# The MLP's last product as rows of tokens, and the context's values inside the mixer's first units

## The reference, cut to what matters

```python
# end of the first block; x is the sum after its mixer
h2 = rms_norm(x, norm_mlp_pre)
u = relu(h2 @ w_mlp_in)                                  # 1024 -> 4096
x = x + rms_norm((u * u) @ w_mlp_out, norm_mlp_post)     # 4096 -> 1024
# second block
mod, mod_k = silu(c) @ mod_w + mod_b, silu(c_ctx) @ mod_w + mod_b   # shift, scale, gate
hk = rms_norm_2(ctx, norm_g) * (1 + scale_k) + shift_k   # 256 context tokens
h = rms_norm_2(x, norm_g) * (1 + scale) + shift          # 1024 tokens
vk = hk @ w_in[:, :512]                                  # the context's values
_, state_k = rglru(vk, lp, 0)                            # gives only a start state
y, _ = mix(h, lp, state_k, pool_grid)                    # four branches, then w_out
x = x + gate * y
return rms_norm_2(x, final_g)
```

## Time and profile before

| what | us |
|---|---|
| median of 3 runs | 3014.23 |
| the profiled execution, its own time | 3017.82 |
| its span | 3016.0 |
| TensorE busy | 2786.5 (92%) |
| VectorE busy | 1413.4 (47%) |
| ScalarE busy | 954.2 (32%) |
| mean granted TensorE clock | 0.967 |

### The profile page before, as it was taken

The page is one execution under the profiler, slowest core; times in us unless marked ns, Lnnn a source line. Parts: engine busy times, 40 slices in busy tenths (PEclk is TensorE's granted clock), DMA queues, the critical chain, the costliest instruction groups (busy, mean ns, idle before and its releaser), DMA issues. The chain is left out here.

```text
span 3016.0 us, 35043 instructions
## 1 busy us (share of the span) xinstructions
PE 2786.5 (92%) x14772; PEld 2166.3 (72%) x14772; DVE 1413.4 (47%) x1638; ACT 954.2 (32%) x1324; POOL 121.4 (4%) x185
## 2 busy tenths in 40 slices
PE   6999998999989899999999999998499989998987
PEld 5867776666756676678888888886377778867776
DVE  2165443344142235944434343234647678842943
ACT  4142112243122445533324232121445622223022
POOL 0001110000000200100111100000000000000000
PEclk9989999999999999999999999998699999999999
DMA  2121101111111103642333322112221121113231
GB/s 102 42 73 40 33 30 47 62 40 31 47 48 60 50 27 98 206 159 70 98 95 93 112 85 86 47 49 84 87 67 49 36 70 56 49 42 123 77 123 65
DMA packets 67399, 215.68 MB, mean 72 GB/s; under 512 B 7752, under 2 KB 12648, under 8 KB 66736
## 3 DMA queue, kind: packets, MB, share of 16 engines
q1 hardware_dynamic: 52848, 159.76, 16.4%
q0 software_dynamic: 14400, 53.75, 5.2%
HBM read 177.83 MB, written 35.65 MB: 71 GB/s over the span
## 5 line engine op out<-in xcount | busy, mean ns | idle before, releaser
L281 PE MATMUL psum<-mixer_in,weights_parts 128*128 128x512 f32 x2112 | 504.2, 399 | 19.3 <-PEq L184 16.3
L281 PEld LDWEIGHTS psum<-mixer_in,weights_parts 128*128 128x128 f32 x2112 | 398.1, 189 | 118.7 <-issue 17.8
L439 PE MATMUL psum<-hidden,weights_parts 128*128 128x512 f32 x1536 | 436.4, 426 | 32.3 <-ACT early_gate L463 14.6
L439 PEld LDWEIGHTS psum<-hidden,weights_parts 128*128 128x128 f32 x1536 | 288.1, 196 | 116.3 <-issue 32.3
L248 DVE TENSOR_TENSOR weights_parts<-weights_raw,weights_parts 128x1024 fp32r<-128x1024 f32 (+2 forms) x186 | 200.4, 1077 | 355.9 <-ACT weights_parts L232 355.9
L281 PE MATMUL psum<-mlp_hidden,weights_parts 128*128 128x512 f32 x1536 | 352.2, 391 | 0.0
L281 PEld LDWEIGHTS psum<-mlp_hidden,weights_parts 128*128 128x128 f32 x1536 | 288.5, 188 | 63.1
L281 PE MATMUL psum<-mlp_in,weights_parts 128*128 128x512 f32 x1440 | 330.4, 391 | 0.5 <-DVE weights_parts L248 0.5
L281 PEld LDWEIGHTS psum<-mlp_in,weights_parts 128*128 128x128 f32 x1440 | 270.4, 188 | 60.0 <-DVE weights_parts L248 0.9
L281 PE MATMUL psum<-hidden,weights_parts 128*128 128x512 f32 x1200 | 277.5, 393 | 8.8 <-PEq L633 3.4
L232 ACT CAST weights_parts<-weights_raw 128x1024 fp32r<-128x1024 f32 (+2 forms) x186 | 172.9, 930 | 324.5 <-PE psum L281 244.9
(11 more groups left out here) (464 smaller groups left out, 3192.1 us busy)
## 6 DMA issues: line engine op xcount, KB each, us to landing
weights_raw<-in_w_in SPq DMA_DIRECT2D x73, 512.0 KB, 3.6
weights_raw<-in_w_mlp SPq DMA_DIRECT2D x64, 512.0 KB, 3.6
mod_weights<-in_mod_w POOLq DMA_DIRECT2D x80, 256.0 KB, 3.7
weights_raw<-in_w_gate SPq DMA_DIRECT2D x32, 512.0 KB, 3.7
gate_scratch<-early_gate SPq DMA_DIRECT2D x64, 256.0 KB, 2.0
gate<-gate_scratch POOLq DMA_DIRECT2D x32, 512.0 KB, 3.9
weights_raw<-in_w_out SPq DMA_DIRECT2D x20, 512.0 KB, 3.7
x_tokens<-in_x SPq DMA_DIRECT2D x4, 1024.0 KB, 8.1
```

The source lines that it names most:

```text
L281: mm = nc.tensor.matmul(c.psum[:, bank + h, 0:cols], c.parts[:, s, wp, at], moving(k, xp, h), start=(n < halves), stop=(n >= halves * (3 * ...
L439: mm = nc.tensor.matmul(c.psum[:, bank, :], c.parts[:, s, wp, at], self.hidden[:, k, xp, h * HALF:(h + 1) * HALF], start=(k == 0 and n == ...
```

## The change

The MLP's `gemm` ends after 56 units, with the hidden channels of the fourth chunk, which now lie in `mixer_in`. The last eight units become `mlp_rows`, a block in the form of `merged_rows`: the product in rows of tokens, and beside it the sum with `y` (turned back by TensorE, "own", copied by ScalarE, and added by VectorE), the post norm, the residual, the store, the pre norm, the turn to channels ("turn"), the modulation ("moved", eight operations of 128x128 in PSUM) and the two parts of the mixer's input. The rows overwrite the columns of `mixer_in` that they came from. The first token half of the mixer's units 0 and 1 is multiplied at the end of the block. `context_values` and `add_residual` go. The context is normed at the head of `project_and_recur`, turned between the second halves of units 0 and 1, and its product is made behind each of the units 0 to 3. The recurrence's gate weights are loaded in two halves. `mixer_out` only adds and gates; the final residual is added in rows in `final_norm`, where the squares are summed too.

In `gemm`, for units 0 and 1 that were begun in the block before:

```diff
+def second_halves():
+    last = [second_half(0)]
+    if between:
+        between(pe)
+    last.append(second_half(1))
+    for u in range(2):
+        mm = beside(pe, u) if beside else last[u]
+        mm.then_inc(c.unit_done, 1)
```

In `mlp_rows` the weights' splitting, the loads (the residual's rows go through three slots) and `mean_square` (square with a running sum, then root) are as in `merged_rows`. `inverse` waits for the root and takes the reciprocal; `normed` is a ScalarE copy scaled by it. Where the turns stand in TensorE's program, SP's loop, ScalarE's and VectorE's programs, and TensorE's waits:

```diff
+at = {(2, 3): [("turn", 0)], (2, 6): [("own", 2)], (2, 7): [("turn", 1)]}
+for b in range(3, BLK):
+    at[b, 6], at[b, 7] = [("own", b)], [("turn", b - 1)]
...
+for b in blocks:
+    if b == BLK - 1:
+        sp.wait_ge(vecs.sem, vecs.value(f"sum{b}"))
+        sp.dma_start(y[:, 4:6, :], t["ctx"].rearrange("(b p) d -> p b d", p=P)).then_inc(
+            c.ctx_loaded, 16)
+    sp.wait_ge(vecs.sem, vecs.value(f"added{b}"))
+    store(c, sp, t["x_second"][:, b, :], rows(b))
+    if b + 3 < BLK:
+        sp.wait_ge(c.scratch_stored, c.stored)
+        sp.wait_ge(act.sem, act.value(f"normed{b}"))
+        load(b + 3)
+sp.wait_ge(c.scratch_stored, c.stored)
...
+def turned_high(b):
+    a.wait_ge(vecs.sem, vecs.value(f"moved{b}"))
+    nc.scalar.copy(hidden[:, :, 0, columns(b)], turned(b)).then_inc(
+        act.step(f"high{b}"), 1)
...
+def own_rows(b):
+    a.wait_ge(pes.sem, pes.value(f"own{b}"))
+    nc.scalar.copy(y[:, :, columns(b)], turned(b)).then_inc(
+        act.step(f"own{b}"), 1)
+def norm_first(b):
+    a.wait_ge(vecs.sem, vecs.value(f"sum{b}"))
+    mean_square(1, b, result(b), w[:, 0, 0, :])
+def norm_second(b):
+    a.wait_ge(vecs.sem, vecs.value(f"added{b}"))
+    mean_square(2, b, rows(b), w[:, 0, 0, :])
...
+for b in blocks:
+    if b > 1:
+        own_rows(b)
+    norm_first(b)
+    if b > 1:
+        turned_high(b - 1)
+    if b == BLK - 2:
+        a.wait_ge(pes.sem, pes.value("parts_free"))
+        next_high(0)
+    norm_second(b)
+    if b == 1:
+        turned_high(0)
+    a.wait_ge(vecs.sem, vecs.value(f"inverse2_{b}"))
+    nc.scalar.activation(normed, rows(b), ACT.Copy,
+                         scale=rstd[:, 1, b:b + 1]).then_inc(
+                             act.step(f"normed{b}"), 1)
+    if b == BLK - 2:
+        next_high(1)
+turned_high(BLK - 1)
```

```diff
+def whole(b):
+    v.wait_ge(c.unit_done, u0 + b + 1)
+    v.wait_ge(act.sem, act.value(f"own{b}"))
+    tt(result(b).rearrange("p (k n) -> p k n", k=KT),
+       result(b).rearrange("p (k n) -> p k n", k=KT), y[:, :, columns(b)],
+       ALU.add).then_inc(vecs.step(f"sum{b}"), 1)
+def residual(b):
+    inverse(1, b)
+    stt(result(b), result(b), rstd[:, 0, b:b + 1], gain[:],
+        ALU.mult, ALU.mult).then_inc(vecs.step(f"scaled{b}"), 1)
+    v.wait_ge(x_loaded[b % 3], 16 * (b // 3 + 1))
+    v.wait_ge(vecs.sem, vecs.value(f"scaled{b}"))
+    tt(rows(b), rows(b), result(b), ALU.add).then_inc(vecs.step(f"added{b}"), 1)
+def moved(b):
+    v.wait_ge(pes.sem, pes.value(f"turn{b}"))
+    for k in range(KT):
+        nc.vector.tensor_scalar(turned(b)[:, k, :], turned(b)[:, k, :],
+                                times[:, k, 0:1], plus[:, k, 0:1], ALU.mult,
+                                ALU.add).then_inc(vecs.step(f"moved{b}"), 1)
+def turned_low(b):
+    v.wait_ge(act.sem, act.value(f"high{b}"))
+    tt(hidden[:, :, 1, columns(b)], turned(b),
+       hidden[:, :, 0, columns(b)].bitcast(F32),
+       ALU.subtract).then_inc(vecs.step(f"low{b}"), 1)
...
+v.wait_ge(gain_loaded, 16)
+for b in blocks:
+    whole(b)
+    if b > 1:
+        moved(b - 1)
+    residual(b)
+    if b == 1:
+        moved(0)
+    elif b:
+        turned_low(b - 1)
+    inverse(2, b)
+    if b == 1:
+        turned_low(0)
+    if b == BLK - 2:
+        for s in range(2):
+            low(KT + s, c.parts[:, s, 1, 0:D], c.raw[:, s, 0:D],
+                c.parts[:, s, 0, 0:D])
+moved(BLK - 1)
+turned_low(BLK - 1)
```

```diff
+def own(b):
+    if b >= 2:
+        p.wait_ge(vecs.sem, vecs.value(f"low{b - 2}"))
+    for k in range(KT):
+        last = nc.tensor.transpose(turned(b)[:, k, :], y[:, k, columns(b)],
+                                   c.ident[:])
+    last.then_inc(pes.step(f"own{b}"), 1)
...
+def turn(b):
+    p.wait_ge(act.sem, act.value(f"normed{b}"))
+    for k in range(KT):
+        last = nc.tensor.transpose(turned(b)[:, k, :], normed[:, columns(k)],
+                                   c.ident[:])
+    last.then_inc(pes.step(f"turn{b}"), 1)
...
+own(0)
+own(1)
...
+for b in range(2, BLK):
+    p.wait_ge(vecs.sem, vecs.value(f"added{b - 2}"))
+    for k in range(KT):
+        for kind, n in at.get((b, k), []):
+            do[kind](n)
+        last = product(b, k)
+        if (b, k) == (BLK - 1, 1):
+            last.then_inc(pes.step("parts_free"), 1)
+    last.then_inc(c.unit_done, 1)
...
+for u in range(2):
+    p.wait_ge(c.low_ready, u0 + KT + u + 1)
+    p.wait_ge(vecs.sem, vecs.value(f"added{BLK - 2 + u}"))
+    p.wait_ge(vecs.sem, vecs.value("low3"))
+    for k in range(KT):
+        if u and k == 5:
+            turn(BLK - 1)
+        for n, (wp, xp) in enumerate(((0, 0), (0, 1), (1, 0))):
+            mm(ps[:, 2 * u, :], c.parts[:, u, wp, columns(k)],
+               hidden[:, k, xp, 0:HALF], start=(k == 0 and n == 0),
+               stop=(k == KT - 1 and n == 2))
```

In `project_and_recur` ScalarE and VectorE first do for the context what lines 2916 to 2945 did, with the rows in `y`, and go on with the rate operations. TensorE:

```diff
+def ctx_turn(pe):
+    pe.wait_ge(vecs.sem, vecs.value("ctx_scaled1"))
+    for k in range(KT):
+        for b in range(2):
+            mm = nc.tensor.transpose(ctx_turned(k)[:, b * P:(b + 1) * P],
+                                     ctx_rows[:, b, k * P:(k + 1) * P], c.ident[:])
+    mm.then_inc(pes.step("ctx_turned"), 1)
+def ctx_product(pe, u):
+    if u >= MIX:
+        return None
+    if u >= 2:
+        pe.wait_ge(ctx_kept, u)
+    for k in range(KT):
+        if u == 0:
+            pe.wait_ge(vecs.sem, vecs.value(f"ctx_low{max(k, 1)}"))
+        for n, (wp, xp) in enumerate(((0, 0), (0, 1), (1, 0))):
+            mm = nc.tensor.matmul(c.psum[:, ctx_banks[u], 0:CTX],
+                                  c.parts[:, u % 2, wp, k * P:(k + 1) * P],
+                                  ctx_parts[:, k, xp, :], start=(k == 0 and n == 0),
+                                  stop=(k == KT - 1 and n == 2))
+    return mm
```

```diff
+def scale(act, u, s, result, act_count, dve_count, q, j):
+    act.wait_ge(c.dve_done, dve_count(u))
     nc.scalar.activation(one(final, u), one(y, u), ACT.Copy,
-                         scale=c.vectors[:, bass.ds(u + g0, 1)]).then_inc(c.act_done, 1)
-def add_all(dve, u, s, result, act_count, dve_count, q, j):
+                         scale=gate[:, bass.ds(u, 1)]).then_inc(c.act_done, 1)
+def add(dve, u, s, result, act_count, dve_count, q, j):
     nc.vector.tensor_tensor(one(y, u), one(y, u), result, ALU.add).then_inc(c.dve_done, 1)
```

In `final_norm` TensorE turns blocks 0 to 7 into four pairs of banks, ScalarE takes square and root of each added row; VectorE and SP:

```diff
+v.wait_ge(gain_loaded, 16)
+for b in range(BLK + 1):
+    if b < BLK:
+        v.wait_ge(pes.sem, pes.value("turned", b))
+        v.wait_ge(rows_loaded[b], 16)
+        nc.vector.tensor_tensor(rows[:, b, :], rows[:, b, :],
+                                c.banks(2 * (b % 4)), ALU.add).then_inc(
+                                    vecs.step(f"added{b}"), 1)
+    if b:
+        n = b - 1
+        v.wait_ge(act.sem, act.value("root", n))
+        nc.vector.reciprocal(rstd[:, n:b], ss[:, n:b]).then_inc(
+            vecs.step(f"inverse{n}"), 1)
+        v.wait_ge(vecs.sem, vecs.value(f"inverse{n}"))
+        nc.vector.scalar_tensor_tensor(
+            y[:, n, :], rows[:, n, :], rstd[:, n:b], gain[:], ALU.mult,
+            ALU.mult).then_inc(vecs.step(f"out{n}"), 1)
...
-for b in range(BLK):
-    sp.wait_ge((vecs if b % 2 else act).sem, rows_done(b))
+sp.dma_start(gain[:], t["gain_rows"][3].partition_broadcast(P)).then_inc(
+    gain_loaded, 16)
+for b in blocks:
+    sp.wait_ge(vecs.sem, vecs.value(f"out{b}"))
     store(c, sp, t["out"][b * P:(b + 1) * P, :], y[:, b, :])
```

625 lines of the change are left out of this document (261 added, 364 removed).

## The result

The changed kernel takes 2975.39 us (median of four, 2972.37 to 2978.36) against 3015.07 us before (median of four, 3012.39 to 3017.64): 39.7 us less, ratio 0.9871 with a 95% interval of 0.9859 to 0.9883. The forecast was 2968 with a range of 2955 to 2987 and a chance of 0.93 for faster: time and sign are inside, the middle was 7 us too low. The two profiled executions differ by more than the medians, 3016.0 - 2970.5 = 45.5 us of span: the one of before (3017.82) lay above its median, the one of after (2972.37) was the fastest of its four.

The account below looks back on a forecast made before the run. TensorE mostly waits in the serial chain `add_residual` and `context_values`. Up to unit 2, 165.3 against 212.6 us (-47.3), end +1.5, total -45.8: 2972 for the profiled execution, less 3.6 to the median, 2968; range 2955 to 2987.

Parts of the forecast that it names:

- Blocks 0 and 1: Row stage's first two blocks: 27.8 us, bounds 24 and 33; block 2 starts at 30.8, after block 0's norm chain.
- Block 2: Irregular row block: 12.8 + 0.9 for two turns + 3.0 waiting at "own" for block 0's low part = 16.7 us.
- Period: Row blocks 3 to 7: 12.8 us each, 10.98 for the product plus sixteen transposes, if two waits are met.
- Rival B: Row blocks: per-block chain longer than the block's product, 1 to 3 us per block for six blocks, 2974 to 2986; chance 0.20.
- Rival F: Mixer's head: context's part stays exposed; 2.4 in the sum, wholly exposed 8 more, 2976; chance 0.04.
- Stage: Whole row stage to the next block's start: product ends at 111.7, then 15.5 for the end, 127.2 us.
- Head: Mixer's start up to unit 2: 23.2 us, including a new 4.6 wait for the weights' split behind the rate operations.
- Clock: Slow clock after four stops (block 2's start, its "own", the barrier, unit 2): 4 us together, between 0 and 7.
- Rival C: New stretch up to unit 2: clock stays up over the stops, -50 to -54, 2960 to 2964; chance 0.12.
- Rival E: Row stage: a stop in each block keeps the clock at its lower level; +49, 3063, slower; chance 0.04.
- rival D: Mixer units 3 to 12: recurrence started late, its gate products make TensorE wait; miss of 10 to 20, 2978 to 2988; chance 0.06.
- End: Last product -3.9, start of final block -2.5, final block of 33 us 7.9 lost: +1.5 together.

Follow-up runs that it names:

- the padded kernel: Changed kernel with an unused 32-byte tile per partition before y, so y and mixer_in start at a multiple of 64 bytes: 2957.36 us, ratio to before 0.9825.
- the doubled operations: Changed kernel with eight more VectorE operations of the "moved" kind in each row block, results into an unused tile: 3003.84 us.

## Why the prediction came out as it did

The mechanism was right and its sum up to unit 2 was within 0.3 us (-47.3, measured -47.6, the context's products behind units 2 and 3 included). Single terms were off by up to 1.1 us, to both sides, so 0.3 is in part luck. Step by step:

- **Gap after the last hidden unit**: 5.2, measured 5.07.
- **Blocks 0 and 1**: block 2 at 30.8, measured 29.7 (stop 3.0, measured 2.78); the table load stood in the chain as said, and taking it out moved the start by 1.3.
- **Block 2**: 16.7, measured 16.8, but with a wait of 1.31 and 12 slow matmuls where I had a wait of 3.0 and the slow clock beside it. They are the same time seen twice: a slow start hides under the wait for the low part.
- **Period**: 12.8, measured 12.94, and 12.77 in the padded kernel; "moved" 0.33 each, above the 0.281 that I took, inside the bounds. Room ahead of "own" 0.6, measured 0.5 to 0.6. Rival B's mechanism is real, as the doubled operations show, and did not occur. Rival F named 8 for the context wholly exposed; by itself it cost 8.9.
- **Stage**: 127.2, measured 127.9. **Head**: 23.2, measured 24.3, with a stop of 3.8 for the 4.6 forecast and slow second halves (7.38 for 5.5); 1.8 of the 24.3 is slow clock, which the sum priced by itself. **Context's products** behind units 2 and 3: 2.98 each for 2.85.
- **Clock**: 4 us priced; the slow 24 matmuls lose 1.8, unit 2 1.8, the 12 of block 2 1.6, and the last lies under a wait. How many stops have it differs between executions of the same code, so this term has a spread of its own, some 1 to 2 us. Rival C (the clock stays up) fell here. Rival E's mechanism, slow clock by repeated stops, is what made the doubled operations cost 29 us rather than 16; the changed kernel has no stop from block 3 to 7, so it does not meet it.
- **Mixer, units 3 to 12**: +1.2, of 10 to 20 that rival D asked for. Rival D fell.
- **End**: the last product -3.9 as forecast (stop 0.71 for 0.9). The final block was mis-sized: 33 forecast, 29.3 measured. The first output was done at 9.1 for 9.7 (the gain had landed at 3.6 for 4.0); the period is 2.53 for 2.75, which makes 1.3 by the last row; and 3.4 us, not 5.1, lie behind it.

Two things were not in it. The first is the hidden channels' move into `mixer_in`: 5.2 us in the MLP's units, which no sentence of the forecast mentions, though the diff moves their operand and the trace of before has units of 10.98 and of 11.20 side by side. In the profiled execution, whose time was forecast as 2972 and is 2972.37, it nearly cancels with the final block (-3.8), the -2.1 from run to run and the mixer's +1.2: that the sum agrees to 0.4 is luck. The second is the step from the profiled execution to the median: I took 3.6 off, because the one of before lay so far above its median; the one of after lies 3.0 below its own. These two, with the 0.4, are the 7 us. A single profiled execution carries a spread of this size: the stretch before the row stage is the same code in all kernels without the 32 bytes, and it ended between 2005.3 and 2011.2 in their traces.

The Trainium skill (SBUF — State Buffer, section "Operand start alignment") asks of an operand that it start at a multiple of its element size, and says that this is about what is legal, "not speed". Both places of `mixer_in` obey it; on speed the runs here show a difference, 2% of each unit.

## What to carry to other kernels

Compare the length of the same product over every operand that it reads: where one operand's units are 2% off in every trace, with no wait in them, suspect its address and try a pad; 32 bytes were worth 13 us here by the trace and 18 by the median. If the 2% comes and goes between executions, it is something else. Look also at what a change does to the place of a tile whose code it leaves alone. A chain that is covered by half a microsecond is cheap until it isn't: past the cover each stop costs itself and, in most cases, nearly as much again in slow clock; and of two waits in a row only the sum counts, so that filling or shortening the first moves time into the second until both are gone.
